# Two-block transformer on one core: three weight blocks of the first expert in idle buffers, and block sums at the head of a feed-forward pair

## The chip, the core and the metric

The kernel runs on one core of a Trainium2 chip. Times are device microseconds (us) of one execution of the whole program; the time before is the median of three runs. The core has TensorE (PE, matmul), VectorE (DVE), ScalarE (ACT), GpSimd (POOL) and SyncE (SP). SP and POOL compute nothing here, they issue transfers (DMA) from HBM.

## The reference

Everything is float32, one batch of 256 tokens (and 256 context tokens), 1024 channels. The first block has two layers (attention, then a SwiGLU feed-forward of 2816 hidden channels); the second has a gated linear-recurrence mixer and an expert-choice mixture of 16 experts. Cut to the two places that the change touches:

```python
# first block, layer 1: only x goes on, the context rows are not needed any more
x = x + mx[:, 5] * rmsnorm(swiglu(hx, ffn_w13[l], ffn_w2[l]), norm_g[l, 3])   # silu(hx@w1) * (hx@w3) @ w2

# second block
def moe_expert_choice(h, router_w, w_gate, w_up, w_down):
    cap = CAPACITY_FACTOR * T // N_EXPERTS                    # 2 * 256 // 16 = 32 tokens for each expert
    aff = softmax(h @ router_w)
    gate, idx = lax.top_k(swapaxes(aff, 1, 2), cap)           # each expert takes its 32 best tokens
    xs = h[bidx, idx]
    hid = silu(einsum('becd,edf->becf', xs, w_gate)) * einsum('becd,edf->becf', xs, w_up)
    ye = einsum('becf,efd->becd', hid, w_down) * gate[..., None]
    return zeros_like(h).at[bidx, idx].add(ye)
x = x + g_f * moe_expert_choice(h2, router_w, w_gate, w_up, w_down)   # 16 x (1024x2048, 1024x2048, 2048x1024)
return rmsnorm_2(x, final_norm_w)
```

## The kernel before

**Weights.** All weights come in blocks of up to 2 MB (128 partitions x 4096 numbers) through a ring of six slots. A list of jobs, made while the program is built, sets the order: attention weights, feed-forward, and so on, and at the end, for each of the 16 experts, four blocks of w_gate, four of w_up (names `("gu", e, 0..7)`) and four of w_down (`("dn", e, 0..3)`): 192 blocks for the experts. Each job takes the slot that was given out longest ago. SP walks the list in order: it waits until the block that lay in the slot has been used (`weights_used`, raised by PE's first matmul of the next block) and issues the transfer (L2331). Nothing overtakes on SP.

**Before the experts.** The last blocks before them are branch_a, branch_b and two of w_out_2 (`pe_gates`). The blocks `gu 0 0` to `gu 0 5` of the first expert take the six slots as these free up; the seventh and all later ones wait for PE to use blocks of the first expert itself.

**Routing.** `pe_route`, `act_route` and `dve_route` compute the affinities, each expert's 32 best tokens (a chain of small DVE instructions on 16 partitions, L2009 to L2054), and the selection matrix PICK. `pe_xs` gathers the tokens of four experts (one group g) into XS by matmuls with PICK; ACT copies them (L1960).

**Experts.** `pe_experts`: for each expert, 8 blocks of gate and up (16 matmul instructions each, 512 columns), then the transposes of the hidden rows (L2153), then 4 blocks of down. In the first expert, between up and the transposes, PE also runs `pe_first_expert`: the gathers of the other three groups, the transposes of the gate matrix (L2084) and of x (L2091), and the spread of the output gate over the partitions. DVE multiplies gate by up (L2187) and scales the result (L2198).

**Feed-forward pairs.** Most of w13 is multiplied by a Strassen-like scheme (class `Pairs`): two blocks of 128 hidden channels at a time ("a pair": the gate rows and the up rows), seven products instead of eight, in the order 1, 2, 6, 7, 5, 4, 3, each four matmuls into a PSUM bank of its own (seven banks in rotation). Products 6, 7, 5 and 3 need sums of weight blocks (S2, the changed A21, S1, S4), which DVE makes in `dve_blocks` (L950 to L953, each 128x512). PE waits for them ahead of product 6 (`blocks_ready`). DVE adds the products up as they come (L977, L979, L983, L985, L986, L990, L993), with the gating multiplies (L962) between, and frees each bank by that. Layer 0 has 18 pairs of 256 columns (`pairs0`), layer 1 has 20 of 128 columns (`pairs1`). In `Pairs.dve` the sums for pair p+1 stand in pair p behind the two adds of product 5 and ahead of that of product 4.

**Buffers.** AR is one tile of 15360 numbers a partition, cut anew in each stage; X and H hold 512 columns each, of which the right half is free once the context is no longer needed.

Of the kernel before, what the change touches and what calls it, by code (L numbers as in the profile page):

```python
# [23 lines left out]
P = 128  # L24
D = 1024
KD = D // P
TX = 256
# [22 lines left out]
SLOTS = 6  # L50
SLOT = 4096
# [97 lines left out]
def build(nc, A, tab_f, tab_m, vrows, out):  # L149
    es = ExitStack()  # L150
    with es:
# [46 lines left out]
        slot_loaded = [sem(f"slot_loaded{i}") for i in range(SLOTS)]  # L198
# [58 lines left out]
        def job(label, *dmas):  # L257
            s = min(range(SLOTS), key=lambda a: last_in[a])
            slot_of.append(s)
            after.append(int(last_in[s]))  # L260
            last_in[s] = job_at[label] = len(jobs)
            jobs.append(dmas)

# [67 lines left out]
        for e in range(NE):  # L331
            for i in range(8):
                w = A[("expert_w_gate_2", "expert_w_up_2")[i // 4]][0, e]
                job(("gu", e, i), runs(w, (i % 4) * 256, (i % 4 + 1) * 256))
            for i in range(4):
                job(("dn", e, i), runs(A["expert_w_down_2"][0, e], i * 512, (i + 1) * 512))
        loads = [0] * SLOTS
# [30 lines left out]
        def weights(pe, label):  # L368
            j = job_at[label]
            pe.wait_ge(slot_loaded[slot_of[j]], loaded_at[j])  # L370
            return ring[:, slot_of[j], :]

# [510 lines left out]
        class Pairs:  # L883
# [81 lines left out]
            def dve(self, c):  # L965
                last = len(self.at) - 1

                def product(p, n):
                    return ps[:, full_of(c.eng, ("p", n, self.l, p)), 0:self.T]

                self.dve_blocks(c, 0)
                for p in range(last + 1):
                    v, u, w = self.C[p % 2], self.V[p % 2], self.W
                    y = self.hid_of(p, self.y)
                    freed(c.eng, ("p", 1, self.l, p))
                    p6 = product(p, 6)
# [954 lines left out]
        XS = ar(4096, KD, NE * CAP)  # L1931
        SGT = ar(8192, 4, TX)
        YE = ar(9216, 4, D)
        AFT, LEFT, HIT = ar(9216, TX), ar(9472, TX), ar(9728, TX)
        OVER, EVEN, TOP = ar(9984, TX), ar(10240, TX), ar(10496, 4, 8)
        PLACE, CNT = ar(10528, 4, 8), ar(10560, 8)
        DIAG = ar(10752, KD, P)
# [19 lines left out]
        def act_xs(c, g):  # L1957
            for half in range(2):
                b = full_of(c.eng, ("xs", g, half))
                c.free(S.activation(XS[:, 4 * half:4 * half + 4, g * P:(g + 1) * P],  # L1960
# [46 lines left out]
        def dve_route(c):  # L2007
# [55 lines left out]
            for t in range(2):  # L2063
                p3 = PICK[:, t, :].rearrange("p (e s) -> p e s", e=NE)
                g3 = PICKG[:, t, :].rearrange("p (e s) -> p e s", e=NE)
                ins = V.tensor_tensor(g3, p3, aff3[:, t, :].unsqueeze(2).broadcast_to([P, NE, CAP]), ALU.mult)
                (c.mark(ins, pick_ready, 3) if t else c.step(ins))
            for half in range(2):
                ins = V.tensor_tensor(DIAG[:, 4 * half:4 * half + 4, :], ident.unsqueeze(1).broadcast_to([P, 4, P]),
                                      MOD[:, 2, 40 + 4 * half:44 + 4 * half, 0:1].broadcast_to([P, 4, P]), ALU.mult)  # L2070
                c.mark(ins, amp_ready, half + 1)
# [38 lines left out]
        def dve_first_expert(c):  # L2110
            for half in range(2):
# [19 lines left out]
        def pe_experts(pe):  # L2131
            for e in range(NE):
                for half, name in enumerate(("hg", "hu")):
# [4 lines left out]
                    for i in range(4):  # L2138
                        w = weights(pe, ("gu", e, 4 * half + i)).rearrange("p (k n) -> p k n", k=2)
                        for kk in range(2):  # L2140
                            k = 2 * i + kk
                            for t in range(4):
                                mm(ps[32 * t:32 * t + 32, b, :], XS[:, k, e * CAP:(e + 1) * CAP],
                                   w[:, kk, t * 512:(t + 1) * 512], k == 0, k == 7, b if k == 7 and t == 3 else None)
# [173 lines left out]
        def _(sp):  # L2318
# [5 lines left out]
            for j, dmas in enumerate(jobs):  # L2324
# [13 lines left out]
        def _(pool):  # L2338
# [20 lines left out]
            freed(pool, ("yb", KD - 1))  # L2359
# [84 lines left out]
```

## Time and profile before

| | us |
|---|---|
| median of 3 runs (2529.41 to 2533.87) | 2531.6 |
| profiled execution, its own time | 2527.8 |
| span of its trace, first to last instruction | 2525.8 |
| PE busy | 2053.2 (81%) |
| DVE busy | 759.7 (30%) |
| ACT busy | 443.5 (18%) |

PE is the busiest engine over the whole span, but the span has two parts with different limits: up to about 1587 us most time is PE's, and after it the transfers of the expert weights. The granted TensorE clock was 0.907 of full speed on average. Some matmul records are missing in the trace, so the starts of instructions are used rather than their counts.

### The profile page before, as it was taken

What the parts mean: (1) busy time and instruction counts of PE and PEld (TensorE: products, weight loads), DVE (VectorE), ACT (ScalarE), POOL (GpSimd) and SP (SyncE); (2) the same over time, 40 slices, a digit from 0 to 9 for tenths busy, and PEclk for the clock granted to TensorE, in tenths of its full rate; (3) what the DMA queues carried; (4) which work ended last, traced back from release to release, by engine and by line L of the source; (5) the groups of instructions that cost most, each with busy time, mean ns of one, the idle gap of its engine ahead of it and who ended that gap; (6) DMA issues with size and microseconds to landing.
All of it is one profiled execution on the core that took longest, in us unless ns stands there. A gap on an engine that the chain in (4) does not pass through costs nothing.

```text
span 2525.8 us, 28670 instructions
## 1 busy us (share of the span) xinstructions
PE 2053.2 (81%) x11775; PEld 1285.2 (51%) x11775; DVE 759.7 (30%) x1667; ACT 443.5 (18%) x959; POOL 7.0 (0%) x15
## 2 busy tenths in 40 slices
PE   6998899999999999899999997865566565555555
PEld 3544368888747857898877776411111111111111
DVE  3217734555302555685036523000000000001001
ACT  3004534001011455211132221100000000000000
POOL 0000000000000000000000000000000000000000
PEclk9999999999999999999999988977787777778787
DMA  9557861332222521444622322899999999999996
GB/s 382 197 200 295 316 223 34 100 100 61 77 85 43 167 84 52 130 132 119 219 100 93 115 100 111 360 428 428 427 429 427 428 428 428 428 428 427 428 427 284
DMA packets 178514, 614.97 MB, mean 243 GB/s; under 512 B 26096, under 2 KB 119536, under 8 KB 144592
## 3 DMA queue, kind: packets, MB, share of 16 engines
q1 hardware_dynamic: 177568, 610.38, 61.9%
q0 software_dynamic: 816, 2.76, 0.4%
q8 instruction: 94, 1.54, 0.3%
q14 instruction: 36, 0.29, 0.0%
HBM read 612.06 MB, written 1.05 MB: 243 GB/s over the span
## 4 chain that ended last, share of the span: by engine, by line
PE 57%; DMA 33%; DVE 7%; ACT 2%; issue 1%; SPq 0%; DVEq 0%; ACTq 0%
PE ps L360 55%; DMA ring<-in_expert_w_up 14%; DMA ring<-in_expert_w_gate 9%; DMA ring<-in_expert_w_down 8%; PE ps L772 1%; DMA ring<-in_ada_w 1%; DVE AR L950 1%; DVE AR L953 1%; DVE AR L952 1%; DVE ring L951 1%; DVE ST L807 0%; DVE AR L718 0%; DVE X L719 0%; ACT AR L825 0%; ACT AR L837 0%
## 5 line engine op out<-in xcount | busy, mean ns | idle before, releaser
L360 PE MATMUL ps<-ring,AR 128*32 128x256 f32 (+2 forms) x4384 | 581.6, 631 | 360.6 <-DMA ring<-in_expert_w_up 133.5
L360 PEld LDWEIGHTS ps<-ring,AR 128*32 128x32 f32 (+1 forms) x4384 | 197.1, 135 | 719.5 <-issue 246.0
L360 PE MATMUL ps<-H,ring 128*128 128x256 f32 (+2 forms) x2240 | 513.5, 388 | 7.6 <-ACT H L656 5.1
L360 PEld LDWEIGHTS ps<-H,ring 128*128 128x128 f32 x2240 | 403.9, 192 | 103.8 <-issue 55.0
L360 PE MATMUL ps<-AR,ring 128*128 128x256 f32 (+2 forms) x1548 | 358.5, 389 | 3.9 <-DVE AR L962 2.9
L360 PEld LDWEIGHTS ps<-AR,ring 128*128 128x128 f32 x1548 | 273.3, 191 | 84.3 <-issue 53.1
L360 PE MATMUL ps<-AR 128*128 128x128 f32 (+5 forms) x1168 | 171.3, 332 | 25.2 <-ACT AR L825 8.6
L2187 DVE TENSOR_TENSOR AR<-AR,ps 128x512 f32<-128x512 f32 x16 | 11.0, 687 | 585.6 <-PE ps L360 585.6
L360 PEld LDWEIGHTS ps<-AR 128*128 128x128 f32 (+2 forms) x1168 | 126.3, 184 | 56.0 <-issue 47.3
L2198 DVE TENSOR_TENSOR AR<-ps,X 32x256 f32<-32x256 f32 x64 | 26.9, 420 | 280.7 <-PE ps L360 279.0
L2173 ACT ACTIVATE AR<-ps 128x512 f32<-128x512 f32 x16 | 9.6, 597 | 528.4 <-PE ps L360 528.4
L360 PE MATMUL ps<-ring,H 128*128 128x512 f32 (+1 forms) x224 | 76.6, 502 | 0.0
L360 PE MATMUL ps<-ring,SC 128*32 128x512 f32 x576 | 69.1, 606 | 2.8 <-DMA ring<-in_ada_w 2.8
L713 DVE TENSOR_TENSOR H<-H 128x256 f32<-128x256 f32 x21 | 8.9, 425 | 200.9 <-ACT H L699 200.8
L360 PE MATMUL ps<-ring 128*128 128x256 f32 x288 | 68.0, 379 | 0.0
L2179 ACT ACTIVATE AR<-ps 128x512 f32<-128x512 f32 x16 | 9.6, 597 | 326.2 <-PE ps L2153 326.2
L807 DVE TENSOR_REDUCE ST<-ps 128x1 f32<-128x512 f32 (+1 forms) x96 | 57.8, 602 | 25.4 <-PE ps L360 23.2
L825 ACT ACTIVATE AR<-ps,ST 128x512 f32<-128x512 f32 (+1 forms) x96 | 59.2, 617 | 24.2 <-DVE ST L814 21.0
L360 PE MATMUL ps<-H,AR 128*128 128x128 f32 (+2 forms) x320 | 60.5, 333 | 2.4 <-ACT H L617 2.4
L360 PEld LDWEIGHTS ps<-ring 128*128 128x128 f32 x288 | 54.7, 190 | 7.4
L360 PEld LDWEIGHTS ps<-ring,H 128*128 128x128 f32 x224 | 37.5, 191 | 37.8 <-issue 37.7
L934 ACT ACTIVATE AR<-FTAB 128x128 f32<-128x128 f32 (+1 forms) x38 | 13.7, 360 | 226.6 <-DVE FTAB L993 226.6
(284 smaller groups left out, 1443.9 us busy)
## 6 DMA issues: line engine op xcount, KB each, us to landing
ring<-in_expert_w_gate SPq DMA_DIRECT2D x64, 2048.0 KB, 23.4
ring<-in_expert_w_up SPq DMA_DIRECT2D x64, 2048.0 KB, 23.3
ring<-in_expert_w_down SPq DMA_DIRECT2D x64, 2048.0 KB, 23.2
ring<-in_ada_w SPq DMA_DIRECT2D x36, 2048.0 KB, 10.1
ring<-in_ffn_w SPq DMA_DIRECT2D x44, 1024.0 KB, 7.7
ring<-in_w_in SPq DMA_DIRECT2D x12, 2048.0 KB, 7.9
ring<-in_ffn_w SPq DMA_DIRECT2D x16, 1408.0 KB, 7.1
ring<-in_ab_w_in SPq DMA_DIRECT2D x4, 2048.0 KB, 16.0
```

What stands on the lines that cost most here:

```text
L360: m = nc.tensor.matmul(out_, lhsT=lhsT, rhs=rhs, start=start, stop=stop)
L772: m = nc.tensor.transpose(ps[:, b, j * P:(j + 1) * P], PR[:, i % 2, u, j * P:(j + 1) * P], ident)
L807: c.step(V.reduce_max(st[:, m:m + 1], ps[:, b, 0:g.nk], axis=AX_X))
L825: c.free(S.activation(PR[:, i % 2, m, 0:g.nk], ps[:, b, 0:g.nk], ACT.Exp, bias=st[:, 2 + m:3 + m], scale=g.scale, accum_out=st[:, 6 + m:7 ...
L934: c.mark(S.activation(TG[:, p % 2, self.y], w, ACT.Silu), silu_ready, self.silu + 2 * p + 2)
L950: c.step(V.tensor_tensor(S1, A21, A22, ALU.add))
L951: c.step(V.tensor_tensor(A21, A11, A21, ALU.subtract))
L952: c.step(V.tensor_tensor(S2, S1, A11, ALU.subtract))
L953: c.mark(V.tensor_tensor(S4, A12, S2, ALU.subtract), blocks_ready, self.block_base + p + 1)
L2173: c.free(S.activation(GT, ps[:, b, :], ACT.Silu), ("hg", e))
L2187: c.free(V.tensor_tensor(HS, GT, ps[:, b, :], ALU.mult), ("hu", e))
L2198: ins = V.tensor_tensor(YE[32 * q:32 * q + 32, g, t * TX:(t + 1) * TX], ps[32 * t:32 * t + 32, b, 0:TX], GFR[32 * t:32 * t + 32, t, :], AL ...
```

## The change

**Part A, expert weights.** Three of the first expert's blocks, `gu 0 5`, `gu 0 6` and `gu 0 7` (the last three of w_up), no longer go through the ring but to three spare places: two in AR (offsets 9216 and 3072) and one in the right halves of H and X. They stay in the same place of SP's list. Ahead of the first SP waits until DVE has read the last product of branch_a, ahead of the second until YA is complete. What lay at these places is moved: XS is cut into four tiles, the routing's scratch goes to FTAB, DIAG to 9216. PICKG and DIAG, which DVE made ahead of the first expert, are now made in it, behind the gate-by-up multiply. The load of the final norm's weights on POOL waits until that multiply too.

**Part B, pairs.** `dve_blocks(c, p + 1)` stands at the head of pair p.

```diff
+SPARE = 3
-        slot_loaded = [sem(f"slot_loaded{i}") for i in range(SLOTS)]
+        slot_loaded = [sem(f"slot_loaded{i}") for i in range(SLOTS + SPARE)]
-        def job(label, *dmas):
-            s = min(range(SLOTS), key=lambda a: last_in[a])
+        def job(label, *dmas, spare=None):
+
+            if spare is None:
+                s = min(range(SLOTS), key=lambda a: last_in[a])
+                after.append(int(last_in[s]))
+                last_in[s] = len(jobs)
+            else:
+                s = SLOTS + spare
+                after.append(-1)
...
+        SPARE_OF = {("gu", 0, 5 + i): i for i in range(SPARE)}
+        SPARE_AT = [[ar(9216 + 2048 * kk, 4, 2, TX) for kk in range(2)], [ar(3072 + 2048 * kk, 4, 2, TX) for kk in range(2)],
+                    [a[:, :, TX:T2].rearrange("p (t a) n -> p t a n", t=4) for a in (H, X)]]
...
+                if ("gu", e, i) in SPARE_OF:
+                    n = SPARE_OF["gu", e, i]
+                    job(("gu", e, i), *((lambda s, n=n, kk=kk: SPARE_AT[n][kk].rearrange("p t a n -> p (t a) n"),
+                                         part.rearrange("(p k) (t n) -> p k t n", k=2, t=8)[:, kk, :, :]) for kk in range(2)),
+                        spare=n)
...
+        def gate_up(pe, e, i):
+
+            n = SPARE_OF.get(("gu", e, i))
+            if n is None:
+                w = weights(pe, ("gu", e, i)).rearrange("p (k n) -> p k n", k=2)
+                return lambda kk, t: w[:, kk, t * 512:(t + 1) * 512]
+            pe.wait_ge(slot_loaded[SLOTS + n], loaded_at[job_at["gu", e, i]])
+            return lambda kk, t: SPARE_AT[n][kk][:, t, :, :]
...
                     y = self.hid_of(p, self.y)
+                    if p < last:
+                        self.dve_blocks(c, p + 1)
                     freed(c.eng, ("p", 1, self.l, p))
...
                     c.free(V.tensor_tensor(u, u, p5, ALU.add), ("p", 5, self.l, p))
-                    if p < last:
-                        self.dve_blocks(c, p + 1)
...
-        XS = ar(4096, KD, NE * CAP)
+        XS = [ar(a, KD, P) for a in (7168, 4096, 5120, 6144)]
-        DIAG = ar(10752, KD, P)
+        DIAG = ar(9216, KD, P)
...
                 if after[j] >= 0:
                     sp.wait_ge(weights_used, after[j] + 1)
+                if s == SLOTS:
+                    freed(sp, ("ya", KD - 1))
+                if s == SLOTS + 1:
+                    sp.wait_ge(y_ready, KD)
...
-            freed(pool, ("yb", KD - 1))
+            freed(pool, ("hu", 0))
             pool.dma_start(FWR, A["final_norm_w_2"].rearrange("(o a n) -> o a n", o=1, a=4).broadcast_to([P, 4, TX])
```

The order on SP around the first expert, before (each row is one or more transfers; in brackets what the first of them waits for, or each of them where there are several):

```order
L2331 DMA ring<-in_w_out_2 128x8x512 [waits weights_used] x2
L2331 DMA ring<-in_expert_w_gate_2 128x4096 [waits weights_used] x4
L2331 DMA ring<-in_expert_w_up_2 128x4096 [waits weights_used] x4
L2331 DMA ring<-in_expert_w_down_2 128x4096 [waits weights_used] x4
L2331 DMA ring<-in_expert_w_gate_2 128x4096 [waits weights_used] x4
```

And of the changed kernel:

```order
L2364 DMA ring<-in_w_out_2 128x8x512 [waits weights_used] x2
L2364 DMA ring<-in_expert_w_gate_2 128x4096 [waits weights_used] x4
L2364 DMA ring<-in_expert_w_up_2 128x4096 [waits weights_used]
L2364 DMA AR<-in_expert_w_up_2 128x2048 [waits bank_free3]
L2364 DMA AR<-in_expert_w_up_2 128x2048
L2364 DMA AR<-in_expert_w_up_2 128x2048 [waits y_ready]
L2364 DMA AR<-in_expert_w_up_2 128x2048
L2364 DMA H<-in_expert_w_up_2 128x8x256
L2364 DMA X<-in_expert_w_up_2 128x8x256
L2364 DMA ring<-in_expert_w_down_2 128x4096 [waits weights_used] x4
```

The last three up blocks wait for no ring slot any more, and the four down blocks behind them take the slots that these would have had.

The order on DVE in a pair of layer 1, before (from the add of product 3 of the pair ahead to that of this pair; `AR<-ring 128x512` is the first of the four sums):

```order
L993 TENSOR_TENSOR FTAB<-FTAB,ps 128x128
L977 TENSOR_TENSOR FTAB<-FTAB,ps 128x128
L979 TENSOR_TENSOR FTAB<-FTAB,ps 128x128
L962 TENSOR_TENSOR AR<-AR 128x128
L983 TENSOR_TENSOR FTAB<-FTAB,ps 128x128
L985 TENSOR_TENSOR AR<-FTAB,ps 128x128
L986 TENSOR_TENSOR FTAB<-FTAB,ps 128x128
L950 TENSOR_TENSOR AR<-ring 128x512
L951 TENSOR_TENSOR ring<-ring 128x4x128
L952 TENSOR_TENSOR AR<-AR,ring 128x512
L953 TENSOR_TENSOR AR<-ring,AR 128x512
L990 TENSOR_TENSOR FTAB<-FTAB,ps 128x128
```

And of the changed kernel (its lines 977 to 980 are the four sums, its L1006 the add of product 6):

```order
L1020 TENSOR_TENSOR FTAB<-FTAB,ps 128x128
L977 TENSOR_TENSOR AR<-ring 128x512
L978 TENSOR_TENSOR ring<-ring 128x4x128
L979 TENSOR_TENSOR AR<-AR,ring 128x512
L980 TENSOR_TENSOR AR<-ring,AR 128x512
L1006 TENSOR_TENSOR FTAB<-FTAB,ps 128x128
L1008 TENSOR_TENSOR FTAB<-FTAB,ps 128x128
L989 TENSOR_TENSOR AR<-AR 128x128
L1012 TENSOR_TENSOR FTAB<-FTAB,ps 128x128
L1014 TENSOR_TENSOR AR<-FTAB,ps 128x128
L1015 TENSOR_TENSOR FTAB<-FTAB,ps 128x128
L1017 TENSOR_TENSOR FTAB<-FTAB,ps 128x128
```

The four sums moved from behind six small instructions of the pair to ahead of them; nothing was added or dropped.

## Rows read from the trace of the kernel before

**Rows 1.** The page: gigabytes a second in 40 slices, and the chain by line.
```profile
GB/s 382 197 200 295 316 223 34 100 100 61 77 85 43 167 84 52 130 132 119 219 100 93 115 100 111 360 428 428 427 429 427 428 428 428 428 428 427 428 427 284
PE ps L360 55%; DMA ring<-in_expert_w_up 14%; DMA ring<-in_expert_w_gate 9%; DMA ring<-in_expert_w_down 8%; PE ps L772 1%; DMA ring<-in_ada_w 1%; DVE AR L950 1%; DVE AR L953 1%; DVE AR L952 1%; DVE ring L951 1%; DVE ST L807 0%; DVE AR L718 0%; DVE X L719 0%; ACT AR L825 0%; ACT AR L837 0%
```

**Rows 2.** Windows: stretch, PE, PEld, DVE, ACT, POOL busy, clock, DMA share, GB/s.
```profile
1559.00:1587.00 28.00, 15.79 (x93) 10.70 (x95) 16.30 (x45) 5.56 (x11) 0.00 (x0) 0.71 0.00 1
1587.00:1588.00 1.00, 1.00 (x12) 0.31 (x8) 0.00 (x0) 0.00 (x0) 0.00 (x0) 1.00 0.30 66
1600.00:2480.00 880.00, 523.90 (x4032) 162.03 (x4032) 45.15 (x89) 25.09 (x42) 0.00 (x0) 0.79 1.01 428
```

**Rows 3.** Timeline of SP's issues: start, us to the last's end, number.
```profile
1538.16 0.33 SPq L2331 DMA_DIRECT2D ring<-in_expert_w_up  x1
1551.98 0.33 SPq L2331 DMA_DIRECT2D ring<-in_expert_w_up  x1
1586.96 0.33 SPq L2331 DMA_DIRECT2D ring<-in_expert_w_up  x1
1588.68 0.33 SPq L2331 DMA_DIRECT2D ring<-in_expert_w_up  x1
1595.88 0.33 SPq L2331 DMA_DIRECT2D ring<-in_expert_w_down  x1
1602.54 0.33 SPq L2331 DMA_DIRECT2D ring<-in_expert_w_gate  x1
1604.99 0.33 SPq L2331 DMA_DIRECT2D ring<-in_expert_w_gate  x1
1624.43 0.33 SPq L2331 DMA_DIRECT2D ring<-in_expert_w_gate  x1
```

**Rows 4.** Timeline of PE in the first expert, with the wait before.
```profile
1584.19 12.53 PE L360 MATMUL ps<-ring,AR 128*32 128x512 f32 x112 [0.95 <-ACT AR L1960]
1600.59 3.64 PE L360 MATMUL ps<-ring,AR 128*32 128x512 f32 x16 [3.87 <-DMA ring<-in_expert_w_up]
1604.16 12.34 PE L360 MATMUL ps<-AR 128*128 128x128 f32 x96
1620.68 0.63 PE L2153 MATMUL ps<-FTAB,AR 128*128 128x128 f32 x4
1622.06 10.55 PE L360 MATMUL ps<-ring,AR 128*32 128x256 f32 x160 [0.75 <-ACT AR L2179]
```

**Rows 5.** Timeline of ACT: copies of the gathered half groups, first, second, last.
```profile
1607.18 0.60 ACT L1960 ACTIVATE AR<-ps 128x512 f32<-128x512 f32 x1 [13.92 <-PE ps L360]
1609.06 0.60 ACT L1960 ACTIVATE AR<-ps 128x512 f32<-128x512 f32 x1 [1.29 <-PE ps L360]
1616.60 0.60 ACT L1960 ACTIVATE AR<-ps 128x512 f32<-128x512 f32 x1 [1.29 <-PE ps L360]
```

**Rows 6.** Timeline of PE in layer 1's pairs.
```profile
1044.37 1.13 PE L360 MATMUL ps<-AR 128*128 128x128 f32 x8 [1.83 <-DVE AR L953]
1084.48 1.13 PE L360 MATMUL ps<-AR 128*128 128x128 f32 x8 [0.20 <-DVE AR L953]
1085.45 1.06 PE L360 MATMUL ps<-AR,ring 128*128 128x128 f32 x8
1089.02 1.95 PE L360 MATMUL ps<-H,ring 128*128 128x128 f32 x16
1091.17 1.13 PE L360 MATMUL ps<-AR 128*128 128x128 f32 x8 [0.20 <-DVE AR L953]
1171.76 1.13 PE L360 MATMUL ps<-AR 128*128 128x128 f32 x8 [0.20 <-DVE AR L953]
```

**Rows 7.** Timeline of DVE in one of them.
```profile
1085.02 0.29 DVE L993 TENSOR_TENSOR FTAB<-FTAB,ps 128x128 f32<-128x128 f32 x1
1086.11 0.29 DVE L977 TENSOR_TENSOR FTAB<-FTAB,ps 128x128 f32<-128x128 f32 x1 [0.80 <-ACT FTAB L928]
1088.15 0.69 DVE L950 TENSOR_TENSOR AR<-ring 128x512 f32<-128x512 f32 x1
1091.06 0.29 DVE L990 TENSOR_TENSOR FTAB<-FTAB,ps 128x128 f32<-128x128 f32 x1
```

**Rows 8.** Timeline of DVE and PE in two neighbouring pairs of layer 0.
```profile
511.19 0.42 DVE L977 TENSOR_TENSOR FTAB<-RS,ps 128x256 f32<-128x256 f32 x1 [3.50 <-PE ps L360]
509.16 1.89 PE L360 MATMUL ps<-ring,AR 128*128 128x256 f32 x8
521.25 1.89 PE L360 MATMUL ps<-ring,AR 128*128 128x256 f32 x8
```

**Rows 9.** DMA issues: tile, queue, number, KB each, median us to landing.
```profile
ring<-in_ffn_w SPq DMA_DIRECT2D x44, 1024.0 KB, 7.7
X<-in_final_norm_w POOLq DMA_DIRECT2D x1, 512.0 KB, 4.9
```

More of the change, by code:

```diff
@@ L255, in build @@
         slot_of, after, last_in = [], [], [s - SLOTS for s in range(SLOTS)]
-        def job(label, *dmas):
-            s = min(range(SLOTS), key=lambda a: last_in[a])
+        def job(label, *dmas, spare=None):
[6 more added lines that the diff above has]
+                after.append(-1)
             slot_of.append(s)
-            after.append(int(last_in[s]))
-            last_in[s] = job_at[label] = len(jobs)
+            job_at[label] = len(jobs)
             jobs.append(dmas)
+        SPARE_OF = {("gu", 0, 5 + i): i for i in range(SPARE)}
+        SPARE_AT = [[ar(9216 + 2048 * kk, 4, 2, TX) for kk in range(2)], [ar(3072 + 2048 * kk, 4, 2, TX) for kk in range(2)],
+                    [a[:, :, TX:T2].rearrange("p (t a) n -> p t a n", t=4) for a in (H, X)]]
         def rows(w, r0, r1, c0, c1):
@@ L333, in build @@
                 w = A[("expert_w_gate_2", "expert_w_up_2")[i // 4]][0, e]
-                job(("gu", e, i), runs(w, (i % 4) * 256, (i % 4 + 1) * 256))
+                part = w[(i % 4) * 256:(i % 4 + 1) * 256, :]
+                if ("gu", e, i) in SPARE_OF:
[3 more added lines that the diff above has]
+                        spare=n)
+                else:
+                    job(("gu", e, i), runs(w, (i % 4) * 256, (i % 4 + 1) * 256))
             for i in range(4):
                 job(("dn", e, i), runs(A["expert_w_down_2"][0, e], i * 512, (i + 1) * 512))
-        loads = [0] * SLOTS
+        loads = [0] * (SLOTS + SPARE)
         loaded_at = []
@@ L1930, in build @@
         PICK, PICKG = ar(2048, 2, 512), ar(3072, 2, 512)
-        XS = ar(4096, KD, NE * CAP)
+        XS = [ar(a, KD, P) for a in (7168, 4096, 5120, 6144)]
         SGT = ar(8192, 4, TX)
         YE = ar(9216, 4, D)
-        AFT, LEFT, HIT = ar(9216, TX), ar(9472, TX), ar(9728, TX)
-        OVER, EVEN, TOP = ar(9984, TX), ar(10240, TX), ar(10496, 4, 8)
-        PLACE, CNT = ar(10528, 4, 8), ar(10560, 8)
-        DIAG = ar(10752, KD, P)
+        spent = FTAB[:, FT["perm_c"][0]:FT["perm_c"][0] + 1352]
+        AFT, LEFT, HIT, OVER, EVEN = (spent[:, a * TX:(a + 1) * TX] for a in range(5))
+        TOP, PLACE = (spent[:, a:a + 32].rearrange("p (a b) -> p a b", a=4) for a in (1280, 1312))
+        CNT = spent[:, 1344:1352]
+        DIAG = ar(9216, KD, P)
         GT, HS, HT = ar(13312, 512), ar(13824, 512), ar(14336, 4, P)
@@ L1959, in act_xs @@
                 b = full_of(c.eng, ("xs", g, half))
-                c.free(S.activation(XS[:, 4 * half:4 * half + 4, g * P:(g + 1) * P],
+                c.free(S.activation(XS[g][:, 4 * half:4 * half + 4, :],
                                     ps[:, b, :].rearrange("p (k s) -> p k s", k=4), ACT.Copy), ("xs", g, half))
@@ L2062, in dve_route @@
                 n += 1
[L2063 to L2071, printed above, removed]
         def pe_first_expert(pe):
@@ L2110, in dve_first_expert @@
         def dve_first_expert(c):
+            for t in range(2):
+                p3 = PICK[:, t, :].rearrange("p (e s) -> p e s", e=NE)
+                g3 = PICKG[:, t, :].rearrange("p (e s) -> p e s", e=NE)
+                ins = V.tensor_tensor(g3, p3, aff3[:, t, :].unsqueeze(2).broadcast_to([P, NE, CAP]), ALU.mult)
+                (c.mark(ins, pick_ready, 3) if t else c.step(ins))
+            for half in range(2):
+                ins = V.tensor_tensor(DIAG[:, 4 * half:4 * half + 4, :], ident.unsqueeze(1).broadcast_to([P, 4, P]),
+                                      MOD[:, 2, 40 + 4 * half:44 + 4 * half, 0:1].broadcast_to([P, 4, P]), ALU.mult)
+                c.mark(ins, amp_ready, half + 1)
             for half in range(2):
@@ L2138, in pe_experts @@
                     for i in range(4):
-                        w = weights(pe, ("gu", e, 4 * half + i)).rearrange("p (k n) -> p k n", k=2)
+                        w = gate_up(pe, e, 4 * half + i)
                         for kk in range(2):
@@ L2142, in pe_experts @@
                             for t in range(4):
-                                mm(ps[32 * t:32 * t + 32, b, :], XS[:, k, e * CAP:(e + 1) * CAP],
-                                   w[:, kk, t * 512:(t + 1) * 512], k == 0, k == 7, b if k == 7 and t == 3 else None)
+                                mm(ps[32 * t:32 * t + 32, b, :], XS[e // 4][:, k, e % 4 * CAP:(e % 4 + 1) * CAP],
+                                   w(kk, t), k == 0, k == 7, b if k == 7 and t == 3 else None)
                         used()
```

## The prediction, as made before the changed kernel had run

> **What bounds the kernel now.** I read the page first: the line of gigabytes a second and the chain by line [rows 1]. From the 26th of 40 slices on the transfer rate stands at 427 to 429 GB/s, and 31% of the chain are transfers of expert weights; before that the rate moves around 100 to 200 and the chain is PE's, with four entries of DVE's block sums at 1% each. So there are two regimes, and a microsecond is worth something different in each. Then I took windows [rows 2]: the transfers stand still from 1559 to 1587 us (share 0.00, 1 GB/s) and run from 1588 on without a hole (share 1.01, 428 GB/s over 1600 to 2480). In this second part the end is set by bytes: how many blocks are still to come when the stream starts, and whether it ever runs dry. In the first part the end is set by PE's path. Then SP's timeline [rows 3], to see what starts each transfer, PE's and ACT's in the first expert [rows 4, 5], and the pairs of both feed-forward layers [rows 6 to 8].
>
> A block is 128 x 4096 x 4 bytes = 2.097 MB; at 428 GB/s [rows 2] that is 4.90 us. Here a page gives another figure: the Trainium skill, "DMA: Bandwidth & Descriptors", section Specifications, puts the HBM limit for a core at about 358 GB/s, which would make a block 5.86 us and the gain of part A worked out below 16.6 instead of 8.9 us. The trace decides for 428.
>
> **Part B, the pairs of layer 1.** In the pairs of 128 columns PE waits for the sums ahead of product 6 in every pair [rows 6]: "0.20 <-DVE AR L953". The first such product starts at 1044.37, the last at 1171.76, 19 periods later; that is 6.70 us a pair (6.69 from 1084.48 to 1091.17). What would PE need without the wait? Four products start between 1085.45 and 1089.02, 0.893 us each, so seven take 6.25. The difference is larger than the 0.20 shown, as PE's modelled end hides part of it. DVE is what takes 6.69: its pair is the small instructions, the sums (1088.15 to 1091.06, 2.91 us) and 0.80 us of waiting for ACT's copy of product 1 (L928), which itself waits behind ACT's silu of the pair ahead [rows 7]. Without the wait DVE works 6.69 - 0.80 = 5.89 us a pair, which is below PE's 6.25.
>
> At the head of the pair the sums lie beside that wait on ACT, and they are done about 3 us after product 3 of the pair ahead (0.3 to notice it, 0.33 for the add L993, 2.91 for the sums), while PE asks for them only one whole pair later. What is late next? The banks: product 2 of the next pair needs the bank that the add L979 of this pair frees. That add now ends about 4.2 us after the product 3 ahead (3.5 and two small adds of 0.33), and is wanted 6.25 + 0.89 = 7.1 us after it: 2.9 us of slack. DVE is in balance with 5.89 against 6.25. So PE runs through: 127.39 - 19 x 6.25 = 8.6 us less. In the first pair the sums for pair 1 delay the adds by 2.9 us; the 2.9 of bank slack covers that barely, and I price it at 0 (at most 0.3). The sums of pair 0, with PE's wait of 1.83 [rows 6], stay. Bounds: 0 if something else holds PE at the same pace, 8.6 as it cannot beat its own products. I take 8.6.
>
> In layer 0 (256 columns) the pair is 12.09 us (509.16 to 521.25) and there is no wait of PE in its row, DVE idles 3.50 in it [rows 8]: moving 2.9 us of sums inside it changes nothing, 0 in its 18 pairs. All that follows layer 1 up to the first expert hangs on PE, so the 8.6 reach the start of the weight stream, and from there the end.
>
> **Part A, the first expert.** Before, six blocks fit the ring ahead of the experts: the fifth is issued at 1538.16, the sixth at 1551.98, and the seventh at 1586.96, when PE has used the first [rows 3]. The idle transfers of 28 us between [rows 2] have room for three blocks (14.7 us). Now, at 1538.16 SP issues the fifth and at once the three spare ones: their waits (the last product of branch_a, YA) are over before, as the two w_out blocks that PE multiplies at 1538 read YA. The four are 8.4 MB, 19.6 us, done by about 1559; `dn 0 0` is issued at 1551.98 in the place of the sixth and is down by about 1564. The spare blocks are cut into 1 KB rows at worst; w13 has such rows too, and two such halves issued together (2 MB) land after 7.7 us [rows 9], so even three at 7.7 are there by 1563, and PE reads the first of them after 1592. Cost 0. Nine blocks are loaded ahead instead of six.
>
> The gain is not three times 4.90 = 14.7, because the stream runs dry now. PE releases the slots of its first five blocks at 1586.96 and then every 1.72 us [rows 3]. Before, eight slots came free in a row (six of these, then 1602.54 and 1604.99), 39.2 us of transfers from about 1588.2, and the next was issued at 1624.43: three us in time. Now only five of the used blocks lay in the ring; the next slot free is that of `dn 0 0`, and PE comes to that only behind the whole of `pe_first_expert`. When? PE's blocks run 1.72 us apart from 1584.19 [rows 3, 4], and all eight are there: the eighth ends at 1584.19 + 8 x 1.72 = 1597.9. Before, PE waited 3.87 for the eighth and ran it and the next gather at half speed, so that the gathers began at 1604.16 [rows 4]. From there to the transposes were 16.5 us (to 1620.68); with the first gather half at the pace of the others (1.88 us apart, against about 2.8 for the first [rows 5]) that is 15.6. Transposes at 1613.5, first down matmul 1.38 later at 1614.9, and the issue 2.37 behind that (1622.06 to 1624.43) at 1617.2. PICKG and DIAG, now in the expert, are four DVE instructions behind the multiply of about 1599, done by 1603; PE wants them behind the gathers, at about 1609. Cover 6 us, cost 0.
>
> So the stream runs from 1588.2 with five blocks (24.5 us) to 1612.7, plus 0.5 MB for the final norm's weights (1.2 us at 428 GB/s [rows 2, 9]), which now load here: 1613.9. The next transfer moves from about 1618.5 (1.2 behind the issue, as 1586.96 and the window of 1587 show). 4.6 us of hole. The norm's load falls into it and costs nothing; without a hole it would cost 1.2. To the end: between the first released slot and the issue after the hole, before 8 blocks less had to follow: 8 x 4.90 = 39.2 us of work for 1617.2 - 1586.96 = 30.3 us. **Gain 8.9 us.** From there on all six slots turn over, as before, and each later expert waits for its bytes. Bounds: 14.7 if there is no hole; 6 if `pe_first_expert` takes the old 16.5 and the release comes two us later still. I take 8.9.
>
> **Sum.** 8.6 + 8.9 = 17.5 us. Profiled span 2525.8 - 17.5 = 2508.3, and 2.0 around it: 2510.3. The median of the runs shown is 3.8 above the profiled execution; on that scale 2531.6 - 17.5 = **2514.1 us**.
>
> **Rivals.**
> 1. The stream doesn't run dry: the whole 14.7 of part A, 2531.6 - 8.6 - 14.7 = 2508.3. For it: that is what 28 idle us promise. Against: after five blocks no slot is free, and 24.5 us are shorter than PE's way to the down blocks (1586.96 to 1617.2). It would need PE there by 1612. 7%.
> 2. The expert stage gives nothing: the hole eats all of the 14.7. It would have to last 14.7, with the release of `dn 0 0` at about 1626 instead of 1617. For it: it is the stage's old date, 1624.43, which would hold if the span of PE from 1597.9 to 1614.9 hung on something other than PE. Against: in the rows there PE has hardly a gap. Then 2531.6 - 8.6 = 2523.0. Together with smaller losses of this kind 10%.
> 3. Part B gives nothing: PE's pace in the pairs comes from another wait that takes the place of the sums (banks freed late, ACT's copy). 2531.6 - 8.9 = 2522.7. For it: DVE has only 0.36 us a pair to spare. 9%.
> 4. Slower: the sums at the head bring DVE to the wait for the next w13 block half a pair earlier, ahead of all adds of the pair at hand, and PE then stands for want of banks. It decides from a landing more than 2.9 us behind the head of the pair. If a whole landing of 7.7 us were exposed each time, 7.7 - 2.9 = 4.8 us for each of layer 1's nine changes of block, 43 us in place of the gain of 8.6, with part A's 8.9 kept: 2531.6 + 43 - 8.9 = about 2566. Against: the ring holds the next blocks several pairs ahead, and no row of the pairs shows a wait on a transfer. 2%.
>
> **How the numbers follow.** My own case 72%; its range is 2511 to 2519, from part A between 6 and 11 and the 2 us or so by which medians of this kernel differ. With rivals 1 to 3 mostly taken in, 2508 to 2522.7. A measurement of this kernel can tell about 0.2%, 5 us. Faster by more than that: cases 1 to 3 and mine, less the case that both parts fail: 0.94. Within 0.2%: 0.04. Slower: 0.02.
>
> **What would show it.** In the changed kernel's profile: the rate near 0 only from about 1555 to 1578 (all of it 8.6 earlier), SP with one up block and six half transfers to AR, H and X in a bunch, PE's eight first blocks without a wait on a transfer; a hole of 4 to 6 us in the stream, about 1605 to 1610, between the fifth and the sixth issue behind the start; after it 428 GB/s to the end. In the pairs of layer 1 a period of 6.25 us, no wait on the sums but in the first pair, and DVE waiting for PE at the add of product 3. In layer 0 still 12.09. I am wrong if the pairs stay at 6.69 or if the hole is missing or longer than 8 us.

## The result, and the profile after

| | before | changed |
|---|---|---|
| median, us | 2531.7 (4 runs, 2529.4 to 2533.9) | 2510.5 (4 runs, 2509.7 to 2512.4) |
| profiled execution, its own time | 2527.8 | 2511.2 |
| span of its trace | 2525.8 | 2508.7 |

The ratio is 0.9924, 95% interval 0.9912 to 0.9936: 16 to 22 us faster. The forecast was 2514.1 (17.5 us), with 2508.0 to 2522.7 as the range. The spans of the two traces differ by 17.1.

The page of the changed kernel, gigabytes a second in 40 slices and the chain by line, which answer to [rows 1]:

```profile
GB/s 380 201 202 282 300 257 34 101 95 52 81 84 39 152 118 35 134 148 116 216 102 84 125 77 234 285 428 428 427 428 428 427 428 427 428 428 428 427 428 309
PE ps L378 58%; DMA ring<-in_expert_w_up 12%; DMA ring<-in_expert_w_gate 10%; DMA ring<-in_expert_w_down 10%; DMA ring<-in_ab_w_in 1%; PE ps L799 1%; DVE ST L834 0%; DVE X L746 0%; DVE AR L745 0%; ACT AR L852 0%; ACT AR L864 0%; DVE H L697 0%; DVE AR L886 0%; PE ps L528 0%; DVE ps L833 0%
```

The four entries of the block sums at 1% each are gone from the chain. The rate shows both sides of part A: 234 instead of 111 in the 25th slice, where three more blocks move, and 285 instead of 360 in the 26th, where the stream of expert weights starts and has a hole (a few us in which nothing moves). The slices of the two pages are cut from spans of different length and don't begin at the same work, so they tell where to look, not how much.

**The pairs of layer 1** (PE's timeline in the changed kernel, answers to [rows 6]; start, us, what, the wait ahead in brackets):

```profile
1047.23 1.13 PE L378 MATMUL ps<-AR 128*128 128x128 f32 x8 [1.83 <-DVE AR L980]
1048.20 1.06 PE L378 MATMUL ps<-AR,ring 128*128 128x128 f32 x8
1053.56 1.06 PE L378 MATMUL ps<-AR 128*128 128x128 f32 x8
1059.81 1.06 PE L378 MATMUL ps<-AR 128*128 128x128 f32 x8
1166.12 1.06 PE L378 MATMUL ps<-AR 128*128 128x128 f32 x8
1172.00 28.33 PE L378 MATMUL ps<-AR,ring 128*128 128x256 f32 x130 [1.25 <-DVE AR L989]
```

Only the first pair waits; from 1059.81 to 1166.12 there are 17 periods of 6.25 us. Its DVE (answers to [rows 7]):

```profile
1052.62 0.69 DVE L977 TENSOR_TENSOR AR<-ring 128x512 f32<-128x512 f32 x1
1055.53 0.29 DVE L1006 TENSOR_TENSOR FTAB<-FTAB,ps 128x128 f32<-128x128 f32 x1
1058.29 0.29 DVE L1020 TENSOR_TENSOR FTAB<-FTAB,ps 128x128 f32<-128x128 f32 x1 [0.21 <-PE ps L378]
1058.62 0.69 DVE L977 TENSOR_TENSOR AR<-ring 128x512 f32<-128x512 f32 x1
```

The wait of 0.80 on ACT is gone and DVE waits for PE, at the add of product 3. In layer 0 the pair is 12.08 us (509.13 to 521.21), as before.

**The first expert.** SP's issues in the changed kernel (answer to [rows 3]):

```profile
1533.37 0.33 SPq L2364 DMA_DIRECT2D ring<-in_expert_w_up  x1
1533.74 2.19 SPq L2364 DMA_DIRECT2D AR<-in_expert_w_up  x4
1535.98 0.47 SPq L2364 DMA_DIRECT2D H<-in_expert_w_up  x1
1536.49 11.37 SPq L2364 DMA_DIRECT2D X<-in_expert_w_up  x1
1547.89 3.49 SPq L2364 DMA_DIRECT2D ring<-in_expert_w_down  x1
1582.36 3.76 SPq L2364 DMA_DIRECT2D ring<-in_expert_w_down  x3
1587.51 2.04 SPq L2364 DMA_DIRECT2D ring<-in_expert_w_gate  x2
1612.97 2.06 SPq L2364 DMA_DIRECT2D ring<-in_expert_w_gate  x2
```

The last of the six half transfers held SP for 11.37 us, where the five ahead of it took 0.4 to 0.7 each, and the first down block behind it for 3.49 instead of 0.33 (11.43 and 3.49 in changed_again). What held SP no run here tells. The half in X landed 20.8 us behind its issue, at 1557.3, the four in AR 10 to 16 us behind theirs; PE comes to the first of these blocks at 1588.17, so nothing waited.

Its PE (answer to [rows 4]):

```profile
1579.59 8.79 PE L378 MATMUL ps<-ring,AR 128*32 128x512 f32 x80 [0.95 <-ACT AR L1988]
1588.17 3.64 PE L378 MATMUL ps<-AR 128*32 128x512 f32 x32
1592.46 1.07 PE L378 MATMUL ps<-X,AR 128*32 128x512 f32 x8
1593.46 11.57 PE L378 MATMUL ps<-AR 128*128 128x128 f32 x96
1609.21 0.63 PE L2182 MATMUL ps<-FTAB,AR 128*128 128x128 f32 x4
1610.59 10.55 PE L378 MATMUL ps<-ring,AR 128*32 128x256 f32 x160 [0.75 <-ACT AR L2208]
```

And windows of it (columns as in [rows 2]):

```profile
1562.00:1583.00 21.00, 10.10 (x66) 7.71 (x70) 10.07 (x29) 1.20 (x2) 0.00 (x0) 0.67 0.00 1
1611.00:1612.00 1.00, 1.00 (x26) 0.61 (x20) 0.00 (x0) 0.00 (x0) 0.00 (x0) 1.00 0.08 33
1612.00:1613.00 1.00, 1.00 (x26) 0.57 (x22) 0.00 (x0) 0.00 (x0) 0.00 (x0) 1.00 0.00 0
1613.00:1614.00 1.00, 1.00 (x24) 0.64 (x20) 0.00 (x0) 0.00 (x0) 0.00 (x0) 1.00 0.44 98
1620.00:2480.00 860.00, 506.00 (x3788) 143.48 (x3784) 42.11 (x83) 19.20 (x31) 0.00 (x0) 0.78 1.01 428
```

The eight blocks are used without a wait. The stream runs dry at about 1610, with 33, 0 and 98 GB/s in the three windows, and from 1614 it fills again: a hole of about 4 us. From the first released slot (1582.36) to the issue behind the hole (1612.97) it is 30.6 us; before it was 37.5 for three blocks more.

**By stages.** The end of the trace is a poor measure here, as stretches that the change doesn't touch differ from one execution to the next. So I cut every trace into stages by the starts of five pieces of PE's work: the first product 6 of layer 0's pairs, the first product 6 of layer 1's, the first w2 matmul of layer 1, the first gate matmul of expert 0, and the last down block. "The expert stage" below is that from the first gate matmul to the last down block. The stretch of layer 0's pairs (583.0 to 583.6) is left out. In us:

| trace | to layer 0's pairs | layer 1's pairs | w2 to first gate | first gate to last down block | rest |
|---|---|---|---|---|---|
| before | 460.7 | 133.34 | 406.5 | 922.8 | 18.8 |
| changed | 464.2 | 124.77 | 407.6 | 913.8 | 15.3 |
| before_again | 465.4 | 133.35 | 409.1 | 922.7 | 16.8 |
| changed_again | 464.4 | 124.77 | 407.5 | 913.3 | 18.4 |
| pairs_only | 462.7 | 124.77 | 407.5 | 923.7 | 18.3 |
| spare_only | 462.8 | 133.35 | 409.0 | 913.6 | 18.9 |
| gather_later | 462.9 | 124.77 | 407.5 | 909.8 | 18.4 |
| gathers_twice | 460.2 | 124.77 | 408.1 | 925.1 | 17.1 |
| later_twice | 462.9 | 124.77 | 407.6 | 918.6 | 17.7 |

The two stages that the change touches give 8.6 and 9.0 us, 17.6 together, where 8.6 and 8.9 were forecast.

### The profile page after: what moved, and what is told of

Read it like the earlier page. It is cut to its first block, busy times and chain, and to the rows that moved or that the text cites. A ratio compares the mean times of both kernels' runs of the same rounds, so it can differ in the third digit from the quotient of the medians.

```text
span 2508.7 us, 28673 instructions
## 1 busy us (share of the span) xinstructions
PE 2052.7 (82%) x11775; PEld 1284.3 (51%) x11775; DVE 760.0 (30%) x1667; ACT 443.6 (18%) x959; POOL 7.0 (0%) x15
## 4 chain that ended last, share of the span: by engine, by line
PE 60%; DMA 34%; DVE 4%; ACT 1%; issue 1%; SPq 0%; DVEq 0%; ACTq 0%
PE ps L378 58%; DMA ring<-in_expert_w_up 12%; DMA ring<-in_expert_w_gate 10%; DMA ring<-in_expert_w_down 10%; DMA ring<-in_ab_w_in 1%; PE ps L799 1%; DVE ST L834 0%; DVE X L746 0%; DVE AR L745 0%; ACT AR L852 0%; ACT AR L864 0%; DVE H L697 0%; DVE AR L886 0%; PE ps L528 0%; DVE ps L833 0%
## 5 line engine op out<-in xcount | busy, mean ns | idle before, releaser
L378 PE MATMUL ps<-AR 128*128 128x128 f32 (+6 forms) x1200 | 175.0, 340 | 19.7 <-ACT AR L852 8.6
L378 PEld LDWEIGHTS ps<-AR 128*128 128x128 f32 (+3 forms) x1200 | 128.7, 184 | 48.8 <-issue 40.2
L378 PE MATMUL ps<-H,AR 128*128 128x128 f32 (+3 forms) x328 | 61.7, 340 | 2.4 <-ACT H L644 2.4
L378 PEld LDWEIGHTS ps<-ring,H 128*128 128x128 f32 x224 | 37.5, 191 | 37.8 <-issue 37.7
L378 PEld LDWEIGHTS ps<-H,AR 128*128 128x128 f32 (+2 forms) x328 | 48.8, 186 | 10.3 <-issue 4.5
```

The costliest lines, as they stand in the source:

```text
L378: m = nc.tensor.matmul(out_, lhsT=lhsT, rhs=rhs, start=start, stop=stop)
```

## The experiments

The first three versions and the last two were timed several times. Each of the others ran once and is read by its stages.

**pairs_only.** The kernel before with the sums at the head (part B).

```diff
                     y = self.hid_of(p, self.y)
+                    if p < last:
+                        self.dve_blocks(c, p + 1)
                     freed(c.eng, ("p", 1, self.l, p))
...
-                    if p < last:
-                        self.dve_blocks(c, p + 1)
```

> The kernel before with part B alone. My theory: a pair of layer 1 takes 6.25 us instead of 6.69, 8.6 us less up to the first expert, and all of it reaches the end, as the weight stream starts that much earlier: about 8.6 us faster than before (2523). Rival (the two parts need each other, or the gain is given back at the stream): under 3 us faster. The stream itself should have no hole, as before.

Measured: median 2522.0 against 2533.1, ratio 0.9954 (0.9942 to 0.9967), 8 to 15 us faster. The pairs take 124.8 us; the expert stage 923.7, within 1 us of before. Part B stands alone, and the gain reaches the end.

**spare_only.** The changed kernel with the sums back behind product 5 (that edit in reverse).

> The changed kernel with part B undone. My theory: 8 blocks' worth of transfers (39.2 us) against about 30.5 us between the first released slot and the issue behind the hole: 8.7 us faster than before (2523), pairs of layer 1 at 6.69 us, a hole of some 5 us in the stream. Rival (the stream doesn't run dry): 14.7 us faster. The two parts alone should add up to the whole, 17.3 us; the timed medians of the whole show 21, and if that is real one of the two must show some 4 us more than this.

Measured: median 2523.2 (five runs, four from 2522.7 to 2524.8 and one at 2515.5), ratio 0.9956 (0.9944 to 0.9969). The pairs are at 133.4 again, the expert stage at 913.6, 9.2 us less than in both traces of before. The rival of 14.7 is out by this stage. The timed gains of the two parts, 11.1 and 9.9, add up to 21.0, the 21.2 of the whole; the stages alone give 17.8. What may lie in the rest is taken up under "The total" below.

**gather_later.** PE's work that no one needs in the first expert, moved to the second.

```diff
-                if e == 0:
-                    pe_first_expert(pe)
+                if e < 2:
+                    pe_first_expert(pe, e)
...
-        def pe_first_expert(pe):
-
+        def pe_first_expert(pe, e):
+            if e == 0:
+                for half in range(2):
+                    b = take(pe, ("gf", half))
+                    pe.wait_ge(amp_ready, half + 1)
+                    mm(ps[:, b, :], ones, DIAG[:, 4 * half:4 * half + 4, :].rearrange("p k n -> p (k n)"), True, True, b)
+                return
...
-                if e == 0:
+                if e == 1:
                     act_first_expert(c)
...
```

> The changed kernel, and PE's gathers of groups 1 to 3, the transposes of the gate matrix and of x (with ACT's copies) moved from the first expert into the second; only the spread of the output gate stays in the first. If the hole comes from PE reaching the first down block late, it goes: dn 0 0 is released some 13 us earlier, the stream runs through at 428 GB/s, and the time falls by the hole, 4 to 5 us against the changed kernel (about 21.5 us against before by the profiles). The 15.5 us of PE in the second expert are covered by the 24 us of transfers in flight. Rival (the hole is the transfer queue's own, or later PE work just moves it to the second expert): no change against the changed kernel.

Measured: median 2508.4, ratio 0.9902 (0.9887 to 0.9918). The window of the stage in gather_later (columns as in [rows 2]):

```profile
1600.00:2480.00 880.00, 524.52 (x4090) 164.25 (x4084) 43.79 (x87) 26.38 (x43) 0.00 (x0) 0.79 1.01 428
```

And PE's timeline around its first down block:

```profile
1595.22 2.54 PE L378 MATMUL ps<-AR,FTAB 128*128 128x512 f32 x4 [3.17 <-DVE AR L2138]
1599.36 10.74 PE L378 MATMUL ps<-ring,AR 128*32 128x256 f32 x144 [0.75 <-ACT AR L2209]
```

Counted from the first gate matmul (1578.11) the down block comes 21.3 us later instead of 31.0, the stream has no hole, and the stage is 4.0 us shorter. The hole's cause is PE's way to the first down block. It was not 13 us earlier as I expected but 9.8, because the spread of the output gate now waits 3.17 us for DIAG on DVE, which in the changed kernel lies beside the gathers. Against the kernel before, the stage is 13.0 us shorter, near the 14.7 of three blocks less 1.2 for the final norm's weights (both estimates of the prediction), which now load inside the stream.

**gathers_twice.** The changed kernel, each gather matmul of groups 1 to 3 twice.

```diff
-                for k in range(4):
+                for k, r in [(k, r) for r in ((0, 1) if g else (1,)) for k in range(4)]:
```

> The changed kernel with each gather matmul of groups 1 to 3 issued twice (into the same bank, the second overwrites the first), some 11.3 us more for PE in the first expert. If every us of PE ahead of the first down block lengthens the hole, the whole is 11.3 us longer than the changed kernel, and the hole about 16 us. Rival (the end is set by bytes, PE's work here is covered): 0 to 3 us longer.

Measured: the stage is 925.1 instead of 913.8, 11.3 us longer, and the whole 2520.9. Its PE:

```profile
1590.56 22.88 PE L378 MATMUL ps<-AR 128*128 128x128 f32 x192
1619.00 7.54 PE L378 MATMUL ps<-ring,AR 128*32 128x256 f32 x132 [0.75 <-ACT AR L2208]
```

The gathers went from 11.57 to 22.88 us, and all of these 11.3 us are in the stage. The transfers now stand still for about 15 us instead of 4. The theory holds in the other direction too: once the stream has run dry, PE's time ahead of the first down block is the kernel's time.

**later_twice.** The same doubling in gather_later.

> gather_later with the gathers of groups 1 to 3 issued twice, as in gathers_twice. There the doubled work cost 11.3 us because it stood ahead of the first down block. If it is only the place that makes it dear, the same work in the second expert costs nothing: from the first gate matmul to the last down block 909.8 us as in gather_later (within 1). Rival (PE's work is on the path wherever it stands, or 27 us of PE in the second expert outlast the transfers in flight): up to 11.3 us longer.

Measured: the stage is 918.6 instead of 909.8, 8.9 us longer. My expectation of nothing was wrong. PE in the second expert of later_twice:

```profile
1643.22 23.45 PE L378 MATMUL ps<-AR 128*128 128x128 f32 x192
1671.82 14.15 PE L378 MATMUL ps<-ring,AR 128*32 128x256 f32 x176 [2.04 <-ACT AR L2209]
```

SP's issues there, and a window between them:

```profile
1641.58 2.80 SPq L2366 DMA_DIRECT2D ring<-in_expert_w_gate  x2
1675.87 0.33 SPq L2366 DMA_DIRECT2D ring<-in_expert_w_gate  x1
```

```profile
1670.00:1671.00 1.00, 0.00 (x0) 0.00 (x0) 0.00 (x0) 0.97 (x2) 0.00 (x0) 1.00 0.00 0
```

From the end of the up blocks to the release of the first down block PE now takes about 33 us (1643.2 to 1675.9, with SP's issue behind it), and the five or six blocks in flight are 24 to 29 us. The stream stands still again, for about 9 us between 1666 and 1678, which is the 8.9 of the stage. So the place does decide, but with a budget: in gather_later the same stretch is some 21 us (from 1642.97 to SP's issue at 1663.8) and free, doubled it is not. I had counted only the gathers against the cover, not the transposes, the copy and the first down block behind them.

**early_copy.** The kernel before, and ACT copies product 1 of the next pair ahead of its wait for product 3.

```diff
-                    b = full_of(c.eng, ("p", 1, self.l, p))
-                    c.free(S.activation(v, ps[:, b, 0:self.T], ACT.Copy), ("p", 1, self.l, p))
...
                     c.mark(S.activation(TG[:, p % 2, self.x], v, ACT.Silu), silu_ready, self.silu + 2 * p + 1)
+                    if p + 1 < len(self.at):
+                        copy(p + 1)
```

> The kernel before, and ACT's copy of product 1 of the next pair taken ahead of its wait for product 3, so that DVE no longer waits 0.80 us for it. By the reading in the prediction (DVE's own sequence, 5.89 us plus that wait, makes the 6.69) a pair of layer 1 falls to 6.25 us. By the rival that the chain of waits suggests (products 6, 7, 5 on PE 2.93, then two adds, then the four sums 2.91, then product 6 again: 2.93 + 0.10 + 0.65 + 2.91 + 0.14 = 6.7) it stays at 6.69.

Measured, PE in early_copy:

```profile
1080.69 1.13 PE L360 MATMUL ps<-AR 128*128 128x128 f32 x8 [0.20 <-DVE AR L957]
1087.37 1.13 PE L360 MATMUL ps<-AR 128*128 128x128 f32 x8 [0.20 <-DVE AR L957]
```

And its DVE (L981 and L989 are the adds of products 6 and 5 there):

```profile
1088.64 0.29 DVE L981 TENSOR_TENSOR FTAB<-FTAB,ps 128x128 f32<-128x128 f32 x1 [0.44 <-PE ps L360]
1090.40 0.29 DVE L989 TENSOR_TENSOR AR<-FTAB,ps 128x128 f32<-128x128 f32 x1 [0.49 <-PE ps L360]
```

The wait on ACT is gone, DVE waits for PE in its stead, twice, and the pair still takes 6.68 us. What set the 6.69 was a loop over both engines: DVE adds product 5 when PE is through with it, then makes the sums, and PE's next product 6 waits for these. The trace of before shows DVE's wait for PE as well, though with no bracket: the add of product 5 starts 0.42 us behind that of product 7, where neighbours are 0.32 to 0.33 apart.

```profile
1087.09 0.29 DVE L983 TENSOR_TENSOR FTAB<-FTAB,ps 128x128 f32<-128x128 f32 x1
1087.51 0.29 DVE L985 TENSOR_TENSOR AR<-FTAB,ps 128x128 f32<-128x128 f32 x1
```

**sums_behind_7.** The kernel before, the sums behind the add of product 7.

```diff
                     c.free(V.tensor_tensor(w, u, p7, ALU.add), ("p", 7, self.l, p))
+                    if p < last:
+                        self.dve_blocks(c, p + 1)
                     p5 = product(p, 5)
```

> The kernel before with the sums behind the add of product 7 instead of behind those of product 5. The loop over PE is then 2.04 + 0.10 + 0.33 + 2.91 + 0.14 = 5.5 us and binds no more; DVE's own sequence with the wait on ACT is 5.83 + 0.80 = 6.6 us. If DVE's sequence binds as soon as the loop doesn't: about 6.6 us a pair. If only the loop counts: 6.25.

Measured, PE in sums_behind_7:

```profile
1083.01 1.13 PE L360 MATMUL ps<-AR 128*128 128x128 f32 x8 [0.21 <-DVE AR L953]
1089.60 1.13 PE L360 MATMUL ps<-AR 128*128 128x128 f32 x8
```

6.59 us a pair: opening the loop alone brings 0.1, and then DVE's own sequence with its 0.80 us of waiting on ACT binds. (The first four pairs still take 6.25 to 6.41, as DVE starts ahead of PE and falls behind only there; layer 1's pairs together are 130.4 us, 3.0 less than before.)

**sums_7_early_copy.** Both edits.

> Both: sums behind the add of product 7 and ACT's copy early. Neither the loop (5.5 us) nor DVE's sequence (5.8 to 6.0) is longer than PE's seven products: 6.25 us a pair, as with the sums at the head. If it stays above 6.5 both accounts miss something.

Measured, PE in sums_7_early_copy:

```profile
1083.51 1.06 PE L360 MATMUL ps<-AR 128*128 128x128 f32 x8
1089.77 1.06 PE L360 MATMUL ps<-AR 128*128 128x128 f32 x8
```

6.26 us, no wait, and layer 1's pairs are 124.8 us as in the changed kernel. So two limits lay 0.1 us apart, and the head of the pair removes both with one edit: the sums leave the loop and stand beside the wait on ACT.

**head_pad4.** The changed kernel with idle copies on DVE.

```diff
+                    if self.l:
+                        for _ in range(4):
+                            c.step(V.tensor_copy(FREED[:, 5 * P:6 * P], ones))
                     p5 = product(p, 5)
```

> The changed kernel with four more copies of 128x128 on DVE in each pair of layer 1, behind the add of product 7. DVE has 5.83 us of its own work a pair now and PE 6.25. At 0.2 to 0.33 us each the copies bring DVE to 6.6 to 7.15 us, and the pair must follow it: 0.4 to 0.9 us a pair, 7 to 17 us in all. Rival (DVE is no longer near the path): 6.25 stays.

Measured, PE in head_pad4:

```profile
1083.54 1.16 PE L378 MATMUL ps<-H,ring 128*128 128x128 f32 x8 [0.36 <-DVE FTAB L1008]
1090.41 1.16 PE L378 MATMUL ps<-H,ring 128*128 128x128 f32 x8 [0.36 <-DVE FTAB L1008]
```

6.87 us: the four copies are 1.02 together, and 5.83 (DVE's own work in a pair) + 1.02 = 6.85. Layer 1's pairs take 136.2 us, 11.4 more than in the changed kernel. DVE's sequence is now the second limit, 0.4 us under PE's, and what PE meets when it is passed is the bank of product 2 (freed by the add L1008), not the sums.

**before_again and changed_again.** Both kernels once more, the changed one timed.

> The kernel before once more, unchanged, for a second trace. If the first trace was a quick execution in stretches that the change doesn't touch (it was 3.8 us under the median), its start of layer 0's pairs comes some 2 us later (462.7 as in three of the other traces, against 460.74), while the pairs of layer 1 (133.3 us from the first product 6 to the next matmul behind them) and the first gate matmul to the last down block (922.8 us) come out the same.

> The changed kernel again, timed beside the next one on the same chip. Stages: 124.8 us for layer 1's pairs, 913.8 us from the first gate matmul to the last down block. By the stages 17.5 us faster than before, by the medians so far 21.

Measured: stages as in the table; changed_again has a median of 2512.4 against 2531.3, ratio 0.9925 (0.9912 to 0.9937). before_again comes to layer 0's pairs at 465.4, even 4.6 us later than the first trace, and its third stage is 409.1 instead of 406.5. The first trace of before was a quick one in just the stretches that the change leaves alone, as expected; both touched stages repeat within 0.1 us for before, and within 0.5 for the changed kernel.

**gather_later_again**, beside changed_again on the same chip.

> gather_later again, timed beside the changed kernel: by the stages 4.0 us faster than it (909.8 against 913.8). Rival (given back elsewhere): the same time.

Measured: median 2509.1 against the changed kernel's 2512.4; ratios to before 0.9909 (0.9895 to 0.9922) and 0.9925 (0.9912 to 0.9937). The intervals overlap, so the times alone don't settle it; the stage, 909.7 against 913.3, does, and the medians differ by 3.4. It is the fastest version here.

## Why the prediction was right, and where not

*Two regimes.* Right: a gain ahead of the stream reaches the end, to within 1 us by the stages (pairs_only), and inside it only bytes and holes count (gathers_twice).

*Part B, 8.6 us.* The size was right: 133.34 - 124.77 = 8.57 us, with PE's 6.25 as the floor. The reason I gave was half wrong. "DVE is what takes 6.69" fell with early_copy: without that wait the pair stayed at 6.68. The chain of waits has the loop: products 6, 7 and 5 on PE (2.93), 0.10 until DVE begins, the two adds of product 5 (0.65), the four sums (2.91), 0.14 until product 6 starts again, together 6.7. DVE's sequence with its wait on ACT, 6.59, was the next limit right below (sums_behind_7). That the size came out right in spite of it was partly luck: the edit takes away both limits, and an edit that only shortened the wait on ACT, which my reason would have advised, brings nothing. The bank slack and the order of the next limits (first PE, then DVE's sequence, seen as the bank of product 2) held (head_pad4). The 0.3 that I gave DVE to notice a product is 0.10 in the rows, measured from PE's modelled end; that adds to the slack. Of the first pair's delay PE shows nothing: 1047.23 to 1053.56 is 6.33, of which 0.08 is the first product's own.

*Layer 0.* Right: a pair still takes 12.08 us. Its pairs start 3.4 us later in the changed trace and layer 1's 2.9 us later, so nothing was lost between.

*Part A.* The spare blocks hid wholly, and the eight blocks ran without a wait. But the way there was not the one in the working: SP began the last spare half 3.1 us behind the fifth block and was held by it until 1547.86, so the first down block could be issued only then, and took 3.49. The working, moved by the 4.8 us between the two traces, has that issue at 1547.2, and the spare blocks down at 1554 instead of 1557.3. These 3 us cost nothing, as PE reads the first of the three at 1588.17. From the first gate matmul to the first down matmul it was 30.7 in the working (1584.19 to 1614.9) and 31.0 in the trace. The interval from the first release to the issue behind the hole was 30.3 in the working and 30.6 measured; the hole was about 4 us. The expert stage gained 9.0 between the first traces, 9.2 in spare_only and 8.9 to 9.5 with the second traces. By the working's own formula the measured 30.6 would give 39.2 - 30.6 = 8.6; where the 0.3 to 0.9 more come from is open.

*The total.* By stages 17.6, by the medians 21.2 (16 to 22). The forecast was put on the scale of the median by adding 3.8 us to the profiled execution, as if all else stayed the same. The third stage, from w2 to the first gate matmul, doesn't: it took 407.5 to 408.1 us in all eight traces whose pairs take 124.8 us, and 409.0 to 409.1 in three of the four whose pairs take 133.3; the fourth, the first trace of before, has 406.5. The granted clock differs in the 58 us from about 92 us behind the stage's start. In before_again:

```profile
1273.80:1331.80 58.00, 55.61 (x220) 43.35 (x221) 16.10 (x30) 22.08 (x39) 0.00 (x0) 0.94 0.32 109
1276.86 44.12 PE L360 MATMUL ps<-H,ring 128*128 128x256 f32 x192 [2.35 <-ACT H L656]
```

In changed_again:

```profile
1264.12:1322.12 58.00, 55.62 (x222) 43.11 (x223) 16.94 (x31) 22.92 (x40) 0.00 (x0) 0.97 0.32 109
1267.17 43.26 PE L378 MATMUL ps<-H,ring 128*128 128x256 f32 x192 [2.35 <-ACT H L683]
```

Both have the same two waits of PE at its start (about 1.5 and 2.4 us). Behind them the clock stood at the lower of its two levels (0.50) from 1276.8 to 1280 in before_again, with 0.56 for the next 2 us, and in changed_again only from 1267.1 to 1270.3, with 0.99 for the next 2. The same 192 matmuls behind them take 44.12 us in the one and 43.26 in the other, so this clock is worth 0.9 us; the other 0.7 of the difference in the stage lies further on. 0.94 stands in all four traces with pairs of 133.3 us (before, before_again, spare_only, early_copy). 0.97 stands in the eight with 124.8, but in sums_behind_7 (130.4) and head_pad4 (136.2) too, so it isn't the shorter pairs as such that bring it. Up to 1.6 us of the gain may thus lie in a stretch that has no step in my working. That the change causes it is not shown: the first trace of before, at 0.94, has the shortest third stage of all. Another 2 us of the difference between medians and stages stay open; they lie within the interval.

*Rivals.* No hole (rival 1): out by the windows from 1611 to 1614. Nothing from the experts (2), nothing from the pairs (3), slower (4): out by the two single parts.

## What to carry to other kernels

More prefetch in front of a stream that is bound by transfers is worth its bytes only as far as the ring can go on refilling: count the slots that come free before the consumer's next long stretch, and compare with that stretch. Here three blocks (14.7 us) brought 9, and moving consumer work that nobody needs yet behind the next few blocks brought another 4, as long as that stretch stayed shorter than what was in flight. When an engine waits a fixed bit in every round of a loop, write the loop down over both engines before blaming the slower one; two limits may lie a tenth of a microsecond apart, and an edit that takes away only one shows nothing (early_copy) or little (sums_behind_7).

## What the runs showed of the hardware that I had not expected

The same stretch of a program can run at a different granted clock from one execution to the next. From 190 to 345 us, far ahead of the change, it was 0.97 in the first trace of before and 0.94 in the second, and the first stage, up to layer 0's pairs, took 460.7 and 465.4 us; over all traces it spread from 460.2 (0.97) to 465.4. That is more than half of what part A brought. A single timing can be as far off: 2524.7 stands among nine of the kernel before with a median of 2531.3. So single executions of this kernel can't be compared by their ends.

A burst of half-block transfers can hold the engine that issues them: SP's sixth such issue took 11.37 us, the next block's 3.49, against 0.33 for a block alone. Here 30 us were to spare; where a transfer behind such a burst is needed soon, that time belongs in the sum.
